# Second feed-forward of a hybrid decoder trunk: one plain f tile ahead of its Strassen units in place of two

## The chip, the cores and the metric

One Trainium2 chip, one of its cores, one launch. The metric is the device time of that core in microseconds (us), the median of several executions. Beside it stands one profiled execution, whose trace the rows below are taken from.

## The reference, cut to what matters

One layer of a decoder trunk on 512 prompt tokens and 64 sample tokens (576 columns in all), in fp32, with D_MODEL = 1024 and D_FF = 2816:

```python
def swiglu(x, w_gu, w_down):
    g, u = jnp.split(x @ w_gu, 2, axis=-1)
    return (jax.nn.silu(g) * u) @ w_down
...
    h = x + 0.5 * swiglu(rms_norm(x, w['g_ffn1']), w['w_ffn1_gu'], w['w_ffn1_down'])
...
    h = h + cross_attend(rms_norm(h, w['g_cross']), mem_k, mem_v, w['w_cq'], w['w_co'])
    h = h + 0.5 * swiglu(rms_norm(h, w['g_ffn2']), w['w_ffn2_gu'], w['w_ffn2_down'])
...
y_prompt = rms_norm(hp, g_final)
```

Only the second feed-forward (`ffn2`) is touched. Its hidden width is 22 tiles of 128, called f tiles here.

## The kernel before, in words

The whole network is one program of five instruction streams (`sync`, `gpsimd`, `tensor`, `scalar`, `vector`) that are written out by hand and meet at semaphores. Activations lie transposed: features on the 128 partitions, 576 tokens along the free axis, 8 chunks (`KD`) of the model width. An fp32 matrix product is made of three fp32r products: every operand is split into a high part (`wh`, `xh`, a copy that rounds to fp32r) and a low part (`wl`, `xl`, the difference), and high x high, high x low and low x high are added up in PSUM.

Weights come in blocks of 1024 x 128, in one order for the whole program (`blocks`); SyncE loads each (`load`) into one of 4 `raw` buffers. For a normal block ScalarE makes `wh` and VectorE makes `wl` (`conv`), and TensorE runs `dense`: 8 chunks x 3 products x 2 halves of 288 columns = 48 matmuls (the line in the profile is that of the helper `mm`, L706). A gate block and an up block belong to each f tile. So a plain f tile is two blocks, 96 matmuls.

In `ffn2` the f tiles behind the first `PLAIN` ones are done as Strassen units. Gate weights, up weights and the two halves of the tokens are combined so that seven products of half the depth take the place of eight: `unit(v)` of TensorE runs A11, S1, A12, S2, S4, A22, S3 with 4 chunks x 3 matmuls each, 84 matmuls of 288 columns. Each unit needs sums of the raw weights. They are made by:

- VectorE, `sum_of`: S1, S2, S4 into PSUM banks 4 to 6 and S3 into SBUF (L2428, L2431, L2438, L2435);
- ScalarE, the high parts: `high_gate` (L1761, A11 and A12 straight from `raw`), `high_sums` (L1769), `high_last` (L1779 and L1781);
- VectorE, the low parts of the sums: `low_sums` (L2444) and `low_last` (L2449);
- GpSimd, the low parts of the straight operands (L694 and L697).

The token side has combinations of its own (`token_sums`, `tokens_high` L1792, `tokens_low` L2458), made once, while the product with `w_co` ahead of `ffn2` runs; the last `tokens_low` is done in the first block of `ffn2`. The scale of the RMS norm, `R`, is also ready only after that block's `rms(3)` (ScalarE L1463 and L1464, VectorE L1946 to L1948).

The 22 f tiles come in three groups of 8, 8 and 6 (`FGROUPS`), each followed by the 8 blocks of its down projection. Before the change the first group is 2 plain tiles and 6 units. In the streams of ScalarE and VectorE the plain blocks are a loop over b: b even multiplies the gate product by `R` (L2494), b odd does the same for the up product (L2500), multiplies by the activation (L2503) and splits the result (L1850, L2509). The preparation of unit 0 hangs on the last plain tile: `high_gate(0)` and the four `sum_of` stand at b = 2 PLAIN - 2, `high_sums(0)` and `low_sums(0)` at b = 2 PLAIN - 1:

```python
                if b % 2 == 0:
                    TTT(two(gs[:]), halves(0), two(R[:]), ALU.mult).then_inc(g_scaled, 1)
                    e.wait_ge(g_scaled, FT + i + 1)
                    e.sem_inc(ps_free, 1)
                    if b:
                        conv(n + 2)
...
                if b == 2 * PLAIN - 2:
                    for j in (S1, S2, S3, S4):
                        sum_of(j, 0)
```

TensorE's unit 0 starts its product A11 when L694 of GpSimd (`lo_a`) is done and the gate product of the last plain tile has been read (`ps_free`), and its product S1 when `low_sums(0)` (`lo_s`) is done. `conv` returns at once for a block that belongs to a unit.

Of the kernel before, what the change touches and what calls it, by code (L numbers as in the profile page):

```python
# [15 lines left out]
KD = D // P  # L16
# [35 lines left out]
def hymba_kernel(nc, A, O, consts):  # L52

    with ExitStack() as ctx:
# [48 lines left out]
        def view(base, at, *dims):  # L103
            n = 1
            for d in dims:
                n *= d
            v = base[:, at:at + n]
            if len(dims) == 1:
                return v
            names = "abcd"[:len(dims)]  # L110
            return v.rearrange(f"p ({' '.join(names)}) -> p {' '.join(names)}",
                               **{k: d for k, d in zip(names[1:], dims[1:])})
# [106 lines left out]
        ROWS = dict(prompt=(1, 2, 4, 5), decode=(3, 6))  # L219
        EXPS = dict(prompt=(4, 8, 13, 17), decode=(9, 18))  # L220
        TURNS = dict(prompt=(1, 2, 3, 5), decode=(4, 6))
        HK, PLAIN = KD // 2, 2
        xg = view(MM, 7168, HK, T)
        tok_h, tok_l = view(ARr, 0, HK, 4, TH), view(ARr, 8 * T, HK, 4, TH)
        tok_hf, tok_f = tok_h.bitcast(F32), view(AR, 8 * T, HK, 4, TH)
# [2402 lines left out]
```

## Time and profile before

| | |
|---|---|
| median of 3 runs | 1312.79 us (1312.44 to 1313.26) |
| the profiled execution | 1314.22 us |
| its span in the trace | 1312.4 us |
| mean granted TensorE clock | 0.998 of full speed |
| TensorE busy | 1290.7 us, 98% of the span |
| TensorE weight loads | 1251.4 us, beside the matmuls |
| VectorE busy | 763.1 us, 58% |
| ScalarE busy | 480.0 us, 37% |
| GpSimd busy | 359.4 us, 27% |
| the chain that ended last | TensorE 93%, VectorE 3%, ScalarE 2% |

The span leaves out about 1.8 us of the execution's own time. Rows name an instruction by line, engine, operation and "out<-in". In this stretch of the program `ARr` and `AR` are one buffer that holds the combined operands and tokens, `gua` holds gate, up and activation, `PS` is PSUM, and `raw` the loaded weights. A wait is shown in brackets in front of the instruction that waited, with the instruction that released it.

### The profile page before, as it was taken

Reading aid. Unit: us, or ns where it says so; the run is one execution under the profiler, and the core shown is the slowest. Engines: PE = TensorE matmul, PEld = TensorE weight load, DVE = VectorE, ACT = ScalarE, POOL = GpSimd, SP = SyncE. Lnnn points to the kernel's source line nnn. Section 1 sums busy time; section 2 is a strip of 40 time slices with the busy share of each in tenths; the row PEclk is TensorE's granted clock in tenths of the full one; section 3 lists DMA queues with packets and bytes.
Section 4 is the critical chain, followed back from the end, with each engine's and each line's share of the span. In section 5 each row is a group of like instructions: output and inputs, shape, how many; then the busy total and the mean of one; then the engine's idle time right before and its main releaser. Section 6 shows DMA issues by size and latency. Waiting matters only on the chain.

```text
span 1312.4 us, 24249 instructions
## 1 busy us (share of the span) xinstructions
PE 1290.7 (98%) x10419; PEld 1251.4 (95%) x10419; DVE 763.1 (58%) x934; ACT 480.0 (37%) x709; POOL 359.4 (27%) x428
## 2 busy tenths in 40 slices
PE   7999999999999999999999999999999999999998
PEld 6999999999999999999999997599999999999997
DVE  3535345653644645648665536568795389737953
ACT  6322122221223423455343313245453245413543
POOL 0000789988901302000002100021330033103321
PEclk9999999999999999999999999999999999999999
DMA  6543222222222352124433546422233233323221
GB/s 174 112 101 98 81 79 83 81 81 82 80 85 70 89 101 64 51 73 131 130 89 106 177 163 255 161 65 81 82 95 96 80 97 91 89 81 97 85 61 72
DMA packets 227147, 130.24 MB, mean 99 GB/s; under 512 B 22241, under 2 KB 221393, under 8 KB 227025
## 3 DMA queue, kind: packets, MB, share of 16 engines
q1 hardware_dynamic: 223168, 123.66, 32.8%
q10 hardware_dynamic: 3872, 5.04, 1.1%
q8 instruction: 82, 1.34, 0.4%
q14 instruction: 25, 0.20, 0.0%
HBM read 121.72 MB, written 5.78 MB: 97 GB/s over the span
## 4 chain that ended last, share of the span: by engine, by line
PE 93%; DVE 3%; ACT 2%; issue 1%; DMA 1%; SPq 0%; DVEq 0%; ACTq 0%
PE PS L706 89%; PE PS L1245 1%; DMA AR<-in_x_prompt 1%; PE PS L781 0%; PE PS L1331 0%; ACT wh L1430 0%; ACT gua L1488 0%; DVE Hs L2123 0%; DVE ARr L2444 0%; PE PS L1223 0%; PE PS L863 0%; PE PS L1196 0%; DVE xl L2449 0%; DVE wl L1904 0%; DVE PS L2428 0%
## 5 line engine op out<-in xcount | busy, mean ns | idle before, releaser
L1430 ACT ACTIVATE wh<-raw 128x1024 fp32r<-128x1024 f32 (+1 forms) x152 | 157.7, 1037 | 522.1 <-PE PS L706 521.9
L706 PE MATMUL PS<-xh,wh 128*128 128x288 f32 x1152 | 254.1, 302 | 0.3 <-DVEq L2496 0.2
L706 PE MATMUL PS<-xh,wl 128*128 128x288 f32 x1152 | 247.1, 296 | 0.0
L706 PE MATMUL PS<-xl,wh 128*128 128x288 f32 x1152 | 246.8, 296 | 0.0
L1904 DVE TENSOR_TENSOR wl<-raw,wh 128x1024 fp32r<-128x1024 f32 (+1 forms) x152 | 197.1, 1297 | 67.1 <-ACT wh L1430 66.3
L706 PE MATMUL PS<-yh,wh 128*128 128x288 f32 x960 | 206.5, 297 | 0.0
L706 PE MATMUL PS<-yh,wl 128*128 128x288 f32 x960 | 205.5, 296 | 0.0
L706 PE MATMUL PS<-yl,wh 128*128 128x288 f32 x960 | 205.5, 296 | 0.0
L706 PEld LDWEIGHTS PS<-xh,wh 128*128 128x128 f32 x1152 | 185.3, 190 | 3.1 <-issue 1.5
L706 PEld LDWEIGHTS PS<-xl,wh 128*128 128x128 f32 x1152 | 185.9, 189 | 0.0
L706 PEld LDWEIGHTS PS<-xh,wl 128*128 128x128 f32 x1152 | 185.9, 189 | 0.0
L706 PEld LDWEIGHTS PS<-yh,wh 128*128 128x128 f32 x960 | 154.4, 189 | 1.3 <-DVE yl L2376 0.8
L706 PEld LDWEIGHTS PS<-yh,wl 128*128 128x128 f32 x960 | 154.7, 189 | 0.0
L706 PEld LDWEIGHTS PS<-yl,wh 128*128 128x128 f32 x960 | 154.7, 189 | 0.0
L497 POOL TENSOR_TENSOR acc<-acc,sq 128x576 f32<-128x576 f32 x31 | 52.4, 1692 | 322.8 <-issue 163.4
L510 POOL TENSOR_TENSOR AR<-AR 128x32 f32<-128x32 f32 (+6 forms) x184 | 116.3, 632 | 14.8 <-POOL AR L623 0.4
L706 PE MATMUL PS<-xh,ARr 128*128 128x288 f32 x480 | 105.9, 296 | 0.1
L694 POOL TENSOR_TENSOR ARr<-raw,ARr 128x1024 fp32r<-128x1024 f32 x20 | 55.1, 2756 | 113.4 <-ACT ARr L1761 113.4
L706 PEld LDWEIGHTS PS<-xh,ARr 128*128 128x128 f32 x480 | 80.3, 188 | 0.4 <-ACT sq L1808 0.4
L706 PE MATMUL PS<-ARr 128*128 128x288 f32 x480 | 70.0, 295 | 3.6 <-DVE ARr L2444 3.6
L706 PE MATMUL PS<-xl,ARr 128*128 128x288 f32 x240 | 70.9, 295 | 0.0
L706 PEld LDWEIGHTS PS<-ARr 128*128 128x128 f32 x480 | 65.5, 188 | 4.3 <-DVE ARr L2444 4.3
(364 smaller groups left out, 1804.1 us busy)
## 6 DMA issues: line engine op xcount, KB each, us to landing
raw<-in_w_ffn_gu SPq DMA_DIRECT2D x88, 512.0 KB, 3.9
raw<-in_w_ffn_down SPq DMA_DIRECT2D x32, 512.0 KB, 3.9
raw<-in_w_in SPq DMA_DIRECT2D x16, 512.0 KB, 4.1
raw<-in_w_ckv SPq DMA_DIRECT2D x16, 512.0 KB, 3.9
raw<-in_w_ffn_down SPq DMA_DIRECT2D x16, 384.0 KB, 3.4
Hs<-in_cache_mem_k SPq DMA_DIRECT2D x6, 1024.0 KB, 6.3
raw<-in_w_out SPq DMA_DIRECT2D x8, 512.0 KB, 3.9
raw<-in_w_cq SPq DMA_DIRECT2D x8, 512.0 KB, 4.3
```

Of the source, the lines that this page charges most:

```text
L497: e.tensor_tensor(acc[:, 0:T], acc[:, 0:T], sq[:, k % 2, :], ALU.add).then_inc(acc_ready, 1)
L510: own(TTT(o, a, b, ALU.mult))
L694: TTT(operands(v, A11, 2, 1), raw[:, n % 4, :].rearrange("p (s x) -> p s x", s=2), operands(v, A11, 2, 0).bitcast(F32), ALU.subtract).then ...
L706: return e.matmul(out, lhsT, rhs, start=start, stop=stop, **kw)
L1245: last = e.transpose(bank(4 + q % 3, P, at=f * M + j * P), KB[b][:, j, at:at + P], ident)
L1430: e.activation(wh[:, n % 2, 0:K * P], raw[:, n % 4, 0:K * P], ACT.Copy).then_inc(w_hi, 1)
L1904: TTT(wl[:, n % 2, 0:K * P], raw[:, n % 4, 0:K * P], wh[:, n % 2, 0:K * P].bitcast(F32), ALU.subtract).then_inc(w_lo, 1)
```

## The change

One number: how many f tiles of the first group are plain.

```diff
@@ -219,7 +219,7 @@
         ROWS = dict(prompt=(1, 2, 4, 5), decode=(3, 6))
         EXPS = dict(prompt=(4, 8, 13, 17), decode=(9, 18))
         TURNS = dict(prompt=(1, 2, 3, 5), decode=(4, 6))
-        HK, PLAIN = KD // 2, 2
+        HK, PLAIN = KD // 2, 1
         xg = view(MM, 7168, HK, T)
         tok_h, tok_l = view(ARr, 0, HK, 4, TH), view(ARr, 8 * T, HK, 4, TH)
         tok_hf, tok_f = tok_h.bitcast(F32), view(AR, 8 * T, HK, 4, TH)
```

The second f tile becomes a unit: the first group is 1 plain tile and 7 units, `FIRST_UNIT` goes from 0, 6, 14, 20 to 0, 7, 15, 21, the two blocks of that tile are no longer split by `conv`, and the preparation of unit 0 moves from b = 2 and 3 to b = 0 and 1.

VectorE, from the last step of `rms(3)` to the third of the four sums, before the change:

```order
L1948 SCALAR_TENSOR_TENSOR R<-gua,R 128x576
L1904 TENSOR_TENSOR wl<-raw,wh 128x1024
L2458 TENSOR_TENSOR ARr<-AR,ARr 128x864
L2494 TENSOR_TENSOR gua<-PS,R 128x576
L2500 TENSOR_TENSOR gua<-PS,R 128x576
L2503 TENSOR_TENSOR gua<-gua 128x576
L1904 TENSOR_TENSOR wl<-raw,wh 128x1024
L2509 TENSOR_TENSOR yl<-gua,yh 128x576
L2494 TENSOR_TENSOR gua<-PS,R 128x576
L2428 TENSOR_TENSOR PS<-raw 128x512
L2431 TENSOR_TENSOR PS<-PS,raw 128x512
L2435 TENSOR_TENSOR AR<-raw 128x512
```

and with the change, from the same step to `low_sums(0)` (L2444) and one row on:

```order
L1948 SCALAR_TENSOR_TENSOR R<-gua,R 128x576
L2458 TENSOR_TENSOR ARr<-AR,ARr 128x864
L2494 TENSOR_TENSOR gua<-PS,R 128x576
L2428 TENSOR_TENSOR PS<-raw 128x512
L2431 TENSOR_TENSOR PS<-PS,raw 128x512
L2435 TENSOR_TENSOR AR<-raw 128x512
L2438 TENSOR_TENSOR PS<-PS,raw 128x512
L2500 TENSOR_TENSOR gua<-PS,R 128x576
L2503 TENSOR_TENSOR gua<-gua 128x576
L2444 TENSOR_TENSOR ARr<-PS,ARr 128x3x512
L2509 TENSOR_TENSOR yl<-gua,yh 128x576
```

Both `wl` splits and one round of L2494, L2500, L2503 and L2509 are gone from here, and the four sums stand right behind the first gate product.

ScalarE, from the last step of its `rms(3)` on, as a difference:

```order
 L1464 ACTIVATE R<-R 128x576
 L1792 ACTIVATE ARr<-AR 128x864
-L1430 ACTIVATE wh<-raw 128x1024
+L1761 ACTIVATE ARr<-raw 128x2x512
 L1845 ACT_TABLE_LOAD
 L1845 ACTIVATE gua<-gua 128x576
-L1430 ACTIVATE wh<-raw 128x1024
+L1769 ACTIVATE ARr<-PS 128x3x512
 L1850 ACTIVATE yh<-gua 128x576
-L1761 ACTIVATE ARr<-raw 128x2x512
-L1845 ACTIVATE gua<-gua 128x576
-L1769 ACTIVATE ARr<-PS 128x3x512
```

`high_gate(0)` (L1761), which GpSimd's L694 waits for, stands where the `wh` of the third block stood, in front of the table load.

## Rows read from the trace of the kernel before

**Rows 1.** Waits of TensorE from 895 to 1265 us (us in total, times, longest).

```profile
PE PS L706 <- DVE ARr L2444: 3.6, 3, 1.7
```

**Rows 2.** Timeline of TensorE (start, length, matmuls, in brackets idle time and releaser).

```profile
916.11 0.51 PE L706 MATMUL PS<-xh,wh 128*128 128x288 f32 x2 [0.22 <-DVEq L2496]
...
928.67 0.30 PE L706 MATMUL PS<-xh,ARr 128*128 128x288 f32 x1
...
932.14 1.85 PE L706 MATMUL PS<-ARr 128*128 128x288 f32 x12 [1.71 <-DVE ARr L2444]
...
940.91 0.53 PE L706 MATMUL PS<-ARr,xh 128*128 128x288 f32 x2 [0.57 <-ACT sq L1808]
```

**Rows 3.** Stretches: length, then busy time of each engine, clock, DMA share, GB/s.

```profile
916.11:928.67 12.56, 12.56 (x96) 12.56 (x97) 6.71 (x9) 5.24 (x6) 2.40 (x1) 1.00 0.36 101
950.00:961.15 11.15, 11.15 (x86) 11.15 (x85) 10.38 (x13) 6.13 (x11) 4.11 (x2) 1.00 0.33 95
```

**Rows 4.** Timeline of VectorE from the scale R to the first low sums.

```profile
912.25 0.76 DVE L1948 SCALAR_TENSOR_TENSOR R<-gua,R 128x576 f32<-128x576 f32 x1
913.04 1.23 DVE L1904 TENSOR_TENSOR wl<-raw,wh 128x1024 fp32r<-128x1024 f32 x1
914.18 1.05 DVE L2458 TENSOR_TENSOR ARr<-AR,ARr 128x864 fp32r<-128x864 f32 x1
915.15 0.75 DVE L2494 TENSOR_TENSOR gua<-PS,R 128x576 f32<-128x576 f32 x1
...
922.63 0.76 DVE L2494 TENSOR_TENSOR gua<-PS,R 128x576 f32<-128x576 f32 x1 [3.13 <-PE PS L706]
...
928.87 0.76 DVE L2500 TENSOR_TENSOR gua<-PS,R 128x576 f32<-128x576 f32 x1 [2.64 <-PE PS L706]
...
930.34 1.75 DVE L2444 TENSOR_TENSOR ARr<-PS,ARr 128x1536 fp32r<-128x1536 f32 x1
```

**Rows 5.** Timeline of ScalarE in the same stretch.

```profile
911.35 1.04 ACT L1430 ACTIVATE wh<-raw 128x1024 fp32r<-128x1024 f32 x1
...
918.23 1.04 ACT L1761 ACTIVATE ARr<-raw 128x1024 fp32r<-128x1024 f32 x1
...
926.27 1.46 ACT L1769 ACTIVATE ARr<-PS 128x1536 fp32r<-128x1536 f32 x1 [2.16 <-DVE PS L2438]
```

**Rows 6.** The page's DMA issues: count, KB each, us to landing.

```profile
raw<-in_w_ffn_gu SPq DMA_DIRECT2D x88, 512.0 KB, 3.9
```

**Rows 7.** Timeline of GpSimd.

```profile
885.40 1.99 POOL L497 TENSOR_TENSOR acc<-acc,sq 128x576 f32<-128x576 f32 x1 [4.41 <-ACT sq L1456]
...
919.35 2.40 POOL L694 TENSOR_TENSOR ARr<-raw,ARr 128x1024 fp32r<-128x1024 f32 x1 [12.84 <-ACT ARr L1761]
```

**Rows 8.** Timeline of VectorE beside the first of them, and 8 us later.

```profile
885.29 0.81 DVE L1937 SCALAR_TENSOR_TENSOR xl<-h,gains,xh 128x576 fp32r<-128x576 f32 x1
886.02 1.69 DVE L2467 SCALAR_TENSOR_TENSOR AR<-h,gains,AR 128x288 f32<-128x288 f32 x1
...
894.25 0.50 DVE L2467 SCALAR_TENSOR_TENSOR AR<-h,gains,AR 128x288 f32<-128x288 f32 x1
```

**Rows 9.** Stretches as in rows 3; the clock stands behind POOL's busy time.

```profile
928.00:932.00 4.00, 2.43 (x19) 2.19 (x17) 3.10 (x3) 1.55 (x3) 0.00 (x0) 1.00 0.35 104
1302.00:1303.00 1.00, 1.00 (x10) 0.97 (x10) 0.34 (x2) 0.27 (x1) 0.00 (x0) 1.00 0.00 0
1304.00:1305.00 1.00, 0.80 (x4) 0.37 (x3) 0.96 (x2) 1.00 (x2) 0.00 (x0) 0.50 0.00 0
```

**Rows 10.** Timeline of TensorE at the start of the program.

```profile
14.01 0.68 PE L706 MATMUL PS<-xl,wh 128*128 128x288 f32 x2
14.49 0.68 PE L706 MATMUL PS<-xh,wl 128*128 128x288 f32 x2
...
20.10 0.43 PE L706 MATMUL PS<-xh,wl 128*128 128x288 f32 x2
```

## Prediction

> **What bounds the kernel now.** I read the engines' shares first: TensorE is busy 98% of the span and has 93% of the chain that ended last, so only two things can move the time here, how many matmuls there are and how long TensorE stands still between them. Then its waits in the second feed-forward. The reader is to see how few they are: three waits for the low sums, L2444, 3.6 us together [rows 1], of which 1.71 us belong to unit 0; then 0.22 us in front of the second plain tile and 0.57 us inside unit 0 for an eviction by ScalarE [rows 2]. Last, the timelines of VectorE, ScalarE and GpSimd from 911 to 932 us, because the change moves the preparation of unit 0 there. What matters is which engine reaches `low_sums(0)` last, since TensorE's product S1 hangs on it.
>
> **The matmuls.** The second plain tile is 96 matmuls in 12.56 us; a unit in the middle of the group takes 11.15 us from one to the next, TensorE busy all of that time [rows 3]. The change swaps one for the other: 12.56 - 11.15 = 1.41 us less. The unit that comes in stands among steady ones; VectorE is busy 10.38 us of its 11.15 us, so it doesn't bound it, and the first and the last unit keep their waits. The Trainium skill ("TensorE: Matmul & The Clock Gate", Back-to-back issue gap) gives an isolated matmul of N columns N / 2.4 + 2.5 ns at full clock, 122.5 ns for 288, from which 12 fewer would be an estimated 1.47 us less. The trace has 131 and 133 ns for one [rows 3], and the sum goes by the trace.
>
> **When unit 0 can start.** Before, unit 0 was prepared beside the second plain tile. Now only what TensorE does up to 915.89 us (916.11 less 0.22, the end of the first tile) covers it. Nothing of it could start much sooner, since the first gate product waits for the scale R, and R comes off VectorE at 913.0 us [rows 4]. I follow the new order from there, in times of the old trace.
>
> 1. ScalarE. L1761 takes the place of the `wh` copy at 911.35 us, same size, 1.04 us [rows 5]. Its input is loaded: a load lands 3.9 us after issue [rows 6], and its buffer was free from the split of the block four places earlier, with three blocks of 48 x 0.133 = 6.4 us between.
> 2. GpSimd. Before, it took up L694 1.12 us after L1761 began (918.23 to 919.35) and needed 2.40 us [rows 5, 7]. Now it asks at 911.35 + 1.12 = 912.47 us, while VectorE is in L1948, which reads two inputs from SBUF [rows 4].
> 3. Who waits for whom there is the term that decides. The trace has the pattern once already: GpSimd's L497 was issued at 885.40 us inside VectorE's L1937 and took 1.99 us, and VectorE's next instruction with two SBUF inputs, L2467, took 1.69 us where it takes 0.50 us 8 us later; it ended at 887.71, 0.32 us after GpSimd [rows 7, 8]. So the instruction under way ends, GpSimd goes first, and VectorE stands still until it is done. By that row GpSimd starts in earnest at 913.0 and ends at 913.0 + 2.40 = 915.4 us.
> 4. VectorE. The split `wl` at 913.04 us is gone, which by itself brings the rest forward by 914.18 - 913.04 = 1.14 us. But L2458, now issued at 913.04, also has two SBUF inputs. It is held until 915.4 and needs 0.8 us more (0.97 us alone, less the 0.18 us that L2467 had behind it). The gate product L2494 so starts at 916.15 us, 1.0 us later than before (915.15) and not 1.1 us sooner. Price of the hold: 2.1 us. Its other end is 0, if VectorE gets in first or the two don't meet. I take 2.1, by the row that has the same two engines in the same order.
> 5. TensorE. Before, L2494 at 915.15 released it at 916.11, 0.96 us later [rows 2, 4]. Now A11 of unit 0 starts at 916.15 + 0.96 = 917.1 us: a wait of 1.2 us in place of 0.22.
> 6. The sums. From the start of L2494 to that of L1769 on ScalarE it was 926.27 - 922.63 = 3.64 us, with the same four sums between [rows 4, 5]. Now L1769 starts at 919.8 and ends at 921.25. VectorE does L2500 and L2503 meanwhile (1.5 us, 919.65 to 921.2), whose inputs are ready, so `low_sums(0)` begins at 921.3. From there to TensorE's S1 it was 932.14 - 930.34 = 1.80 us [rows 2, 4]. S1 starts at 923.1 us.
> 7. A11 itself runs 1.76 us (928.67 to 932.14 less 1.71), to 918.9 us. The wait in front of S1 is then 4.2 us in place of 1.71.
>
> **The sum.** From 915.89 us to S1 it was 16.25 us and becomes 7.2, 9.05 us less; the unit that comes in adds 11.15. Net +2.1 us. The same by terms: -1.41 for the matmuls, +1.0 for the first wait, +2.5 for the second. Behind S1 I cost nothing: VectorE, ScalarE and GpSimd go through the same instructions at the same distances from `low_sums(0)`, the 0.57 us wait in unit 0 stays, weights of unit 1 are loaded earlier than before, and the down blocks and the later groups are unchanged but for which of two operand buffers a unit uses.
>
> The profiled execution took 1314.22 us, 1.8 us more than its span and 1.4 more than the median of 1312.79. On its own time the sum gives 1316.3; against the median 1312.8 + 2.1 = **1314.9 us**, 0.16% more. A measurement of this kernel can tell about 0.2%, 2.6 us, from no change.
>
> **Rivals.**
>
> *TensorE's clock falls in the new wait (slower).* The granted clock is 1.00 through the 1.71 us wait [rows 9]. At the end of the program it goes from 1.00 at 1302 us to 0.50 at 1304, that is from 2.4 to 1.2 GHz, after the dense blocks had given way to short transposes and waits [rows 9]. The new stretch from 915.9 to 923.1 has 1.76 us of matmuls and waits of 1.2 and 4.2 us, longer than any other in this trace behind the start. If the clock falls there, S1 and what follows run at half rate for a while. At the start of the program two matmuls took 0.48 us (14.01 to 14.49) where two take 0.26 in the plain tile [rows 3], and the slow pace was over by 20.10 [rows 10]. 6.1 us at that pace cost 6.1 x (1 - 0.133 / 0.24) = 2.7 us, of which the 0.57 us wait in unit 0 can swallow a part: 2.1 us, between ends of 0 and 2.7. Time: 1312.8 + 2.1 + 2.1 = 1317.0, with the upper end at 1317.6. It decides from the point where the sum plus the loss passes 2.6 us, so from a loss of 0.5 us. Against it: I can't tell from the trace how long a wait must be.
> The Trainium skill ("TensorE: Matmul & The Clock Gate", HAM oscillation) says that gaps between bursts of matmuls put the clock back to half, to be earned again, every time. By it this rival would be the rule rather than the exception for 4.2 us. The end of the trace agrees that light work lets the clock fall; no row shows it for a wait of this length between dense matmuls.
>
> *GpSimd and VectorE don't meet (no change).* If L694 is taken up a little later, or VectorE's L2458 gets in first, L2494 starts at 914.0 us, `low_sums(0)` at 919.15, S1 at 920.95, and A11 right at 915.9. Then 16.25 - 5.06 = 11.19 us less against 11.15 more: 1312.8 us. For it speaks that the margin is 0.6 us (912.47 against 913.04); against it the pattern of rows 7 and 8.
>
> *The waits don't grow at all (faster).* Then only the 1.41 us of matmuls show, 1311.4 us. It would need unit 0 to be prepared before R is there, and in the new order the sums stand behind the gate product; I see nothing for it. That the number doesn't do what it says is excluded by the new order, which has seven units in the first group.
>
> **How the numbers follow.** The forecast 0.50, the clock 0.32, no meeting 0.13, other causes 0.05 (mostly further waits in the first two units). The predicted time is that of the forecast, 1314.9. The range takes in the case without the hold at its low end, 1312.5, and the clock at its high end, most of the way to 1317.6: 1317.4. Slower by over 0.2%, above 1315.4: nearly all of the clock's share, and a little of the forecast's and of the rest, 0.37. Within 0.2%: 0.60. Faster by over 0.2% would need 2.6 us where the change removes 1.4 us of matmuls: 0.03.
>
> **What would show it.** Right: GpSimd's L694 for unit 0 at about 912.5 us with about 2.9 us on the record, L2458 beside it with 2.9 to 3.2 us in place of 1.05, L2494 at 916.1, then TensorE waiting about 1.2 us for L2494 and 4.2 us for L2444; seven units with 11.15 us between the middle ones. Wrong: L2458 of about 1.05 us (the hold is no cost), matmuls 0.24 us apart behind S1 with a granted clock under 1.00 (the clock), new waits in units 1 to 6, or a steady unit over 11.15 us.

## The result and the profile after

The changed kernel takes 1315.33 us (median of 11 runs, 1314.46 to 1315.91), the kernel before 1312.55 us in the runs beside it (11 runs, 1310.55 to 1314.99). The ratio is 1.0020, with a 95% interval of 1.0010 to 1.0029: 2.8 us slower, between 1.3 and 3.8. The prediction was 1314.9, 2.1 us slower.

The profiled execution took 1315.53 us, with a span of 1313.7 us. The page's first part, its busy times:

```profile
PE 1288.3 (98%) x10407; PEld 1250.2 (95%) x10407; DVE 770.7 (59%) x940; ACT 484.3 (37%) x715; POOL 362.3 (28%) x430
```

TensorE has 12 matmuls fewer (10407 for 10419) and 2.4 us less busy time (1290.7 before), and the kernel is slower all the same. Its waits from 895 to 1265 us, which answer to [rows 1]:

```profile
PE PS L706 <- DVE ARr L2444: 6.0, 3, 4.1
PE PS L706 <- DVEq L2496: 1.1, 1, 1.1
```

The waits for low sums grew from 3.6 to 6.0 us, all of it in the longest one. The timeline of TensorE at the places of [rows 2]:

```profile
914.94 0.37 PE L706 MATMUL PS<-xh,ARr 128*128 128x288 f32 x1 [1.14 <-DVEq L2496]
...
920.92 3.25 PE L706 MATMUL PS<-ARr 128*128 128x288 f32 x12 [4.15 <-DVE ARr L2444]
```

The two waits are there, 1.14 and 4.15 us. But the twelve matmuls behind the second (product S1) take 3.25 us where they took 1.85: the clock. And the third wait of the rows before, 0.57 us for ScalarE in unit 0, is gone. The stretches around it, read as [rows 9]:

```profile
915.00:918.00 3.00, 1.77 (x12) 1.54 (x12) 2.97 (x5) 0.83 (x2) 0.00 (x0) 1.00 0.00 0
918.00:921.00 3.00, 0.08 (x1) 0.08 (x1) 2.90 (x4) 3.00 (x6) 0.12 (x1) 0.84 0.61 175
921.00:924.00 3.00, 3.00 (x13) 3.00 (x14) 3.00 (x3) 1.04 (x2) 3.00 (x2) 0.50 0.05 13
924.00:927.00 3.00, 3.00 (x14) 3.00 (x14) 3.00 (x3) 0.41 (x1) 1.45 (x1) 0.52 0.58 167
927.00:930.00 3.00, 3.00 (x25) 3.00 (x24) 1.48 (x3) 1.75 (x2) 0.00 (x0) 1.00 0.29 83
```

The columns are as in [rows 3]. TensorE stood still from 916.8 us. In that stillness the granted clock fell to 0.50 (1.2 GHz), was there while 27 matmuls ran in 6 us, and was at 1.00 from 927 us on, where 25 go into 3 us. The mean granted clock was 0.996 or 0.997 in the 11 runs of the changed kernel. In the 66 runs of the kernel before that stood beside the experiments it was 0.997 in 20, 0.998 in 38, 0.999 in 8 and never 0.996, with the change 0.996 in 6 of 11: lower on the whole, but a mean of 0.997 doesn't tell for a single run whether the clock fell here.

What made the wait so long stands on VectorE (first block, as [rows 4]), ScalarE and GpSimd (as [rows 5, 7]):

```profile
910.15 0.76 DVE L1948 SCALAR_TENSOR_TENSOR R<-gua,R 128x576 f32<-128x576 f32 x1
910.95 3.13 DVE L2458 TENSOR_TENSOR ARr<-AR,ARr 128x864 fp32r<-128x864 f32 x1
914.00 0.74 DVE L2494 TENSOR_TENSOR gua<-PS,R 128x576 f32<-128x576 f32 x1
...
919.11 1.76 DVE L2444 TENSOR_TENSOR ARr<-PS,ARr 128x1536 fp32r<-128x1536 f32 x1
```

```profile
909.26 1.05 ACT L1761 ACTIVATE ARr<-raw 128x1024 fp32r<-128x1024 f32 x1
```

```profile
910.38 2.78 POOL L694 TENSOR_TENSOR ARr<-raw,ARr 128x1024 fp32r<-128x1024 f32 x1 [5.97 <-ACT ARr L1761]
```

GpSimd's L694 was issued 0.23 us after VectorE's L1948 had begun, and was done at 913.16, which is 2.25 us after that ended. VectorE's next instruction, L2458, took 3.13 us for 1.05 and ended 0.92 us after GpSimd. What marks the instructions that are held can be read from the same trace: L2431, with one input in PSUM and one in SBUF, took 0.69 to 0.70 us in all 21 units, also beside GpSimd; L2435, of the same size with both inputs in SBUF, took 0.68 us in the fastest and 1.20 in the median.

**A zero point.** In this trace everything up to here happens 2.1 us earlier than in the one of before. The difference is there in full 30 us into the program and stays the same from then on; against the second trace of before (below) the first is off by 1.75 us in the same way, so it belongs to the execution and not to the kernel. What exactly differs in that start was not taken apart. Spans therefore can't be compared to better than some 2 us. From here on times are counted from the mean-square product of `rms(3)`, the last thing both kernels do alike, to the last residual update (L2563). These four rows are its ends, of the kernel before and then of the changed one, from the timelines of TensorE and VectorE:

```profile
906.56 1.29 PE L706 MATMUL PS<-acc,mean_d 128*128 128x512 f32 x4
...
1299.45 0.76 DVE L2563 SCALAR_TENSOR_TENSOR h<-PS,h 128x576 f32<-128x576 f32 x1 [5.44 <-PE PS L706]
```

```profile
904.47 1.29 PE L706 MATMUL PS<-acc,mean_d 128*128 128x512 f32 x4
...
1300.74 0.76 DVE L2563 SCALAR_TENSOR_TENSOR h<-PS,h 128x576 f32<-128x576 f32 x1 [5.44 <-PE PS L706]
```

That is 392.89 us before and 396.27 after, 3.4 us more. The end of the program behind it took between 12.9 and 14.0 us in the traces, whatever the kernel. All traces on this scale, with the ratio of the timed runs to the kernel before:

```
kernel                               to S1   S1 to S2   to last residual   ratio, 95% interval
before                               25.58   3.28       392.89
before, second trace                 25.87   3.29       393.19
changed                              16.45   5.93       396.27             1.0020 (1.0010 to 1.0029)
changed, second trace                16.47   4.83       395.15
e1 gate first                        14.39   4.81       393.08             1.0002 (0.9993 to 1.0011)
e2 28 matmuls in the wait            16.46   3.29       394.99             1.0013 (1.0004 to 1.0022)
e3 both                              14.39   3.29       392.93             0.9997 (0.9988 to 1.0005)
e4 three plain tiles                 38.68   3.28       393.65 (*)         1.0004 (0.9995 to 1.0012)
e5 low sums first (two plain)        24.00   3.18       391.05 (*)         0.9990 (0.9981 to 0.9998)
e5, second trace                     23.98   3.18       392.22
e6 and the eviction first            24.01   3.18       392.22             0.9989 (0.9980 to 0.9998)
e7 sums first (one plain)            12.45   3.27       391.96             0.9994 (0.9985 to 1.0003)
e8 14 matmuls in the wait            16.46   3.27       394.96             1.0015 (1.0006 to 1.0024)
(*) 8 down blocks at 6.24 us each where all others have 6.40: 1.3 us, see the end
```

### The profile page after: what moved, and what is told of

The parts are those of the page before. It is cut to its first block, busy times and chain, and to the rows that moved or that the text cites. A ratio compares the mean times of both kernels' runs of the same rounds, so it can differ in the third digit from the quotient of the medians.

```text
span 1313.7 us, 24248 instructions
## 1 busy us (share of the span) xinstructions
PE 1288.3 (98%) x10407; PEld 1250.2 (95%) x10407; DVE 770.7 (59%) x940; ACT 484.3 (37%) x715; POOL 362.3 (28%) x430
## 4 chain that ended last, share of the span: by engine, by line
PE 94%; DVE 3%; ACT 2%; issue 1%; DMA 1%; SPq 0%; DVEq 0%; ACTq 0%
PE PS L706 90%; PE PS L1245 1%; DMA AR<-in_x_prompt 1%; DVE ARr L2444 0%; PE PS L781 0%; ACT wh L1430 0%; ACT gua L1488 0%; DVE Hs L2123 0%; PE PS L1223 0%; PE PS L863 0%; PE PS L1196 0%; PE PS L1331 0%; DVE ARr L2458 0%; DVE AR L2578 0%; PE PS L874 0%
## 5 line engine op out<-in xcount | busy, mean ns | idle before, releaser
L706 PE MATMUL PS<-xh,wh 128*128 128x288 f32 x1120 | 246.6, 302 | 0.1
L706 PE MATMUL PS<-xh,wl 128*128 128x288 f32 x1120 | 240.2, 296 | 0.0
L706 PE MATMUL PS<-xl,wh 128*128 128x288 f32 x1120 | 239.6, 296 | 0.0
L706 PEld LDWEIGHTS PS<-xh,wh 128*128 128x128 f32 x1120 | 179.8, 189 | 2.5 <-issue 1.1
L706 PEld LDWEIGHTS PS<-xh,wl 128*128 128x128 f32 x1120 | 180.6, 189 | 0.0
L706 PEld LDWEIGHTS PS<-xl,wh 128*128 128x128 f32 x1120 | 180.4, 189 | 0.0
L706 PE MATMUL PS<-xh,ARr 128*128 128x288 f32 x504 | 112.3, 299 | 1.1 <-DVEq L2496 1.1
L706 PEld LDWEIGHTS PS<-xh,ARr 128*128 128x128 f32 x504 | 85.3, 190 | 1.3 <-issue 1.3
L694 POOL TENSOR_TENSOR ARr<-raw,ARr 128x1024 fp32r<-128x1024 f32 x21 | 56.3, 2680 | 109.3 <-ACT ARr L1761 109.3
L706 PE MATMUL PS<-ARr 128*128 128x288 f32 x504 | 74.9, 298 | 6.0 <-DVE ARr L2444 6.0
L706 PEld LDWEIGHTS PS<-ARr 128*128 128x128 f32 x504 | 70.2, 191 | 6.7 <-DVE ARr L2444 6.7
```

The source lines that it names most:

```text
L694: TTT(operands(v, A11, 2, 1), raw[:, n % 4, :].rearrange("p (s x) -> p s x", s=2), operands(v, A11, 2, 0).bitcast(F32), ALU.subtract).then ...
L706: return e.matmul(out, lhsT, rhs, start=start, stop=stop, **kw)
```

## The experiments

The theory after the result: the hold of VectorE by GpSimd costs 2.1 us, which is the whole forecast, since without it the longer wait would cost just what the 12 matmuls give; on top of it comes the fallen clock. The rivals: the hold is harmless, since something else sets S1; and the clock's loss is swallowed by slack.

**e1, gate first.** On ScalarE, `high_gate(0)` of the changed kernel goes in front of `rms(3)`:

```diff
                 if b == 0:
+                    high_gate(0)
                     rms(3)
                     tokens_high(KD - 1)
                 conv(n0 + b + 2)
-                if b == 2 * PLAIN - 2:
-                    high_gate(0)
```

> The changed kernel with one instruction of ScalarE moved: high_gate(0) (L1761) in front of rms(3) and no longer behind tokens_high, so that GpSimd does its L694 before VectorE gets to the scale R. Theory A (the hold costs 2.1 us): L2458 behind R falls from 3.13 to about 1.05 us, the gate product L2494 starts 1.8 us behind R's L1948 where it was 3.85, S1 on TensorE 8.7 us behind L1948 where it was 10.8. The wait in front of S1 becomes about 3.4 us. Against the changed kernel 2.1 us less, 1313.2, if the clock still falls; 3.4 us less, 1311.9 (the time before is 1312.6), if it doesn't. Rival B (the hold was harmless, something else sets S1): L2458 shorter but S1 still near 10.8 us behind L1948, time 1315.3. The hold may turn up in L2467 to L2469, where VectorE has about 2 us to spare.

S1 came 2.06 us sooner, and the last residual 3.2 us sooner than in the first trace of the changed kernel. Against its second trace, in which S1 to S2 takes 4.83 us as it does here (4.81), it is 2.07 us. VectorE's timeline (the experiment's line numbers are 1 less):

```profile
904.29 2.64 DVE L2466 SCALAR_TENSOR_TENSOR AR<-h,gains,AR 128x288 f32<-128x288 f32 x1
...
910.29 1.06 DVE L2457 TENSOR_TENSOR ARr<-AR,ARr 128x864 fp32r<-128x864 f32 x1
911.26 0.75 DVE L2493 TENSOR_TENSOR gua<-PS,R 128x576 f32<-128x576 f32 x1
```

L2458 is back at 1.06 us. The hold didn't vanish, it moved: the token sum now in its way takes 2.64 us for 0.50, in a stretch where VectorE afterwards waits for R anyway. So the hold costs what lies on the path at that moment, and theory A stands. The clock still fell, behind a wait of 3.44 us, but for a shorter time (S1 to S2 4.81 us).

**e2, 28 matmuls in the wait.** On TensorE, between A11 and the wait for S1 of unit 0. They write a bank that nobody reads, so nothing of the computation changes:

```diff
+                if v == 0:
+                    for i in range(28):
+                        mm(bank(0, TH), operand(0, A11, 0)[:, i % HK, :], xh[:, i % HK, lo_t])
                 e.wait_ge(S("lo_s"), 2 * v + 1)
```

> The changed kernel with 28 extra matmuls of 288 columns on TensorE between A11 and the wait for S1 of unit 0, into a bank that nobody reads; they fit in the wait (28 x 0.133 = 3.7 of 4.15 us). Theory A (the fall of the clock costs 1.3 us net): granted clock stays at 1.00 from 915 to 935 us, S1 still 10.8 us behind L1948, S1 to S2 takes 3.3 us where it took 5.9, the 0.57 us wait for ScalarE in unit 0 comes back, and the time is 1.3 us below the changed kernel, about 1314.0. Rival B (the clock's loss is all slack of unit 0): same time as the changed kernel, 1315.3.

The waits of TensorE in its timeline:

```profile
915.85 0.37 PE L706 MATMUL PS<-xh,ARr 128*128 128x288 f32 x1 [1.16 <-DVEq L2499]
...
921.82 1.85 PE L706 MATMUL PS<-ARr 128*128 128x288 f32 x12 [0.41 <-DVE ARr L2447]
...
930.60 0.53 PE L706 MATMUL PS<-ARr,xh 128*128 128x288 f32 x2 [0.56 <-ACT sq L1811]
```

S1 is where it was, and runs in 1.85 us again; the clock is 1.00 in all stretches from 915 to 930 us, and the 0.56 us wait for ScalarE is back. To the last residual it is 1.28 us less than in the first trace of the changed kernel. The timed runs can't tell that from nothing: 1.0013 against 1.0020, with intervals that overlap. What they do say is that the kernel with its clock at full speed is still slower than before: what is left is 2.1 us in the trace, 1.7 (0.5 to 2.9) in the runs.

**e3, both**, with 24 extra matmuls:

> Both edits together, with 24 extra matmuls. Theory A (hold 2.1 us and clock 1.3 us are separate and are all that was lost beyond the swap of 96 matmuls for 84): 3.4 us below the changed kernel, 1311.9, so level with the kernel before at 1312.6 or 0.1 us under it. Rival B (they overlap, or a third wait takes over): more than 1 us above the kernel before.

392.93 us to the last residual, 3.3 below the first trace of the changed kernel and level with the kernel before at 392.89. The two losses add up, 2.06 (e2 to e3) and 1.28 (changed to e2). That it is level, and not below, is the cover that went with the tile: without the hold TensorE stands still for 3.44 us in front of S1 (e1) where it was 0.22 + 1.71, 1.5 us more, as much as the swapped matmuls give.

**e4, three plain tiles**, the opposite step from the kernel before (`PLAIN = 3`):

> The opposite step from the kernel before: three plain tiles ahead of five units. With the preparation of unit 0 covered as before, the waits stay at 0.22, 1.71 and 0.57 us, the clock stays at 1.00 and only the matmuls count: 12.56 - 11.15 = 1.4 us more than before, 1314.0. Rival (the 1.71 us wait of unit 0 is not the same when another tile covers it): not between +0.9 and +1.9 us.

The waits were the same, 0.22, 1.73 and 0.56 us, and the clock stayed up. The runs give +0.5 us (-0.7 to +1.6), in line with 1.4. The trace gives S1 13.10 us later for one unit of 11.15 us less: 1.95 us, more than the forecast, because the two plain tiles between the first and unit 0 took 25.65 us here, 133 ns a matmul, and the one of rows 3 took 12.56, 131 ns. That trace is the only one to have it so: in the other four with two plain tiles the second took as long as here. The total of +0.76 us is about that less 1.3 us for the faster down blocks.

**e8, 14 matmuls in the wait**, e2 with `range(14)`:

> The changed kernel with 14 extra matmuls, 1.9 us of the 4.15 us wait, right behind A11, so that a wait of about 2.3 us is left in front of S1. Theory A (a wait of this length doesn't let the clock fall, as the 1.71 us one did not): clock 1.00 throughout, S1 to S2 3.3 us, and 408.0 us from the mean-square product to the end. Rival B (the two waits together bring it down, whatever stands between): S1 to S2 4.5 us or more.

```profile
920.77 1.85 PE L706 MATMUL PS<-ARr 128*128 128x288 f32 x12 [2.28 <-DVE ARr L2447]
```

With a wait of 2.28 us left, S1 runs in 1.85 us and the clock is 1.00: theory A. In the trace half of the filler does all that the full one does. It is one trace; the mean clock of the 10 timed runs is 0.996 in two of them, 0.997 in seven and 0.999 in one, so it isn't shown that the clock stayed up in each. And the filler did two things, it shortened the wait and gave TensorE more work in front of it; which of them counts was not separated.

**Second traces**, of the kernel before, the changed one and (below) e5:

> The kernel before once more, for a second trace. In the first one the 8 down blocks behind the first group of units took 6.40 us each, in the trace with low_sums(0) moved 6.24 us, although the matmuls are the same. Theory A (each execution falls into one pace or the other by chance): a different pace may show here. Rival B (the pace belongs to the program): 6.40 us again, and 12.56 us for the second plain tile.

> The changed kernel once more. The hold (L2458 at 3.1 us), the wait of 4.15 us in front of S1 and the granted clock of 0.50 behind it come back if they belong to the change and not to one execution: 16.45 us from the mean-square product to S1, 5.9 us from S1 to S2 within 1 us. Theory A on the pace: 6.24 or 6.40 us a down block; rival B: 6.40 again.

The hold (L2458 at 3.14 us), the two waits (1.16 and 4.14 us) and the fall came back. But the clock was low for less long, and it fell only when S1 had begun, at 921.14 us; the stretches as above:

```profile
918.00:921.00 3.00, 0.00 (x0) 0.00 (x0) 2.89 (x3) 3.00 (x5) 0.00 (x0) 1.00 0.62 173
921.00:924.00 3.00, 2.86 (x12) 2.86 (x13) 3.00 (x4) 1.26 (x3) 2.91 (x2) 0.54 0.04 8
924.00:927.00 3.00, 3.00 (x22) 3.00 (x21) 3.00 (x3) 0.41 (x1) 1.67 (x1) 0.89 0.65 174
```

S1 to S2 took 4.83 us for 3.29, a loss of 1.5 us instead of 2.65, and to the last residual it is only 0.16 us more than in e2. So about 1.4 us of the loss are free. Where they go can be read from the starts of S1 of units 0, 1 and 2, at 921.82, 933.88 and 945.43 us in e2 and at 921.14, 933.91 and 945.04 us here. With the clock up the units take 12.06 and 11.55 us and the later ones 11.17, so the first two have 0.9 and 0.4 us more than TensorE needs; here they take 12.77 and 11.13, and 1.25 us of the loss are made up when unit 2 gets to S1. The same shows between e1 and e3, 1.5 us of loss and 0.15 us of price. The second trace of before had the second plain tile at the slower pace (S1 0.29 us later) and down blocks at 6.40 us.

**Can unit 0 be prepared better?** e5 takes the kernel before (two plain tiles) and does `low_sums(0)` right behind the four sums, in front of the last up product:

```diff
-                    if b == 2 * PLAIN - 1:
-                        low_sums(0)
...
                 if b == 2 * PLAIN - 2:
                     for j in (S1, S2, S3, S4):
                         sum_of(j, 0)
+                    low_sums(0)
```

> The kernel before (two plain tiles) with one step of VectorE moved: low_sums(0) (L2444) in front of the last up product L2500, right behind the four sums. Its 1.71 us wait on TensorE should nearly vanish, because L2500 there waits 2.64 us for TensorE with low_sums(0) queued behind it. Theory A (VectorE's queue behind it sets unit 0): S1 starts about 1.6 us sooner, but VectorE gets to the sums of unit 1 only 0.2 us sooner, since it waits for ScalarE's yh; TensorE's wait for ScalarE's eviction L1808 in unit 0 grows from 0.57 to about 2.0 us, and from the mean-square product of rms(3) to the end it is 405.6 us, against 405.8 before. Rival B (the wait in front of S1 is paid in full): 404.2 us and 1.6 us less time.

> The kernel before with low_sums(0) moved, once more. Theory A: the down blocks behind the first group may be at 6.40 us now, and then it is 405.3 us from the mean-square product to the end, 0.5 less than the kernel before. Rival B: 6.24 us again and 404.1 us.

The timeline of TensorE, first trace:

```profile
939.73 0.53 PE L706 MATMUL PS<-ARr,xh 128*128 128x288 f32 x2 [1.61 <-ACT sq L1808]
```

The 1.71 us wait in front of S1 is gone and 1.0 us of it turned up again in front of ScalarE's eviction, which stands in ScalarE's queue behind sums that VectorE makes late: 1.6 us for 0.57. At equal pace (second traces) 0.97 us are left of the gain, and the timed runs confirm a gain: 0.9990 (0.9981 to 0.9998). My 0.2 us was too low, since `low_sums(1)` came 1.0 us sooner (33.35 us behind the mean-square product for 34.33, second traces).

e6 adds, on ScalarE in unit 0, the eviction in front of `high_sums(1)`:

```diff
+                if v == 0:
+                    keep(v, 4, e2, u_bank(v))
                 high_sums(after(v)) if after(v) else conv(units[v] + 3)
-                keep(v, 4, e2, u_bank(v))
+                if v:
+                    keep(v, 4, e2, u_bank(v))
```

> As the one with low_sums(0) moved, and on ScalarE the eviction keep(0, 4) (L1808) of unit 0 in front of high_sums(1) (L1769), so that S3 of unit 0 no longer waits for VectorE's sums of unit 1. Theory A: neither wait is left, S1 of unit 1 waits about 0.5 us for its own low sums, and from the mean-square product to the end it is 403.7 us, 2.1 us less than the kernel before. Rival B (only the eviction's order counted): 0.6 us less, 405.2.

```profile
941.17 1.81 PE L706 MATMUL PS<-ARr 128*128 128x288 f32 x12 [0.67 <-DVE gua L2552]
...
947.27 0.40 PE L706 MATMUL PS<-xh,ARr 128*128 128x288 f32 x1 [1.10 <-ACT sq L1808]
```

Theory A fell. Rival B's number came true against the first trace of before (0.67 us less, 0.6 expected), but not its reason: against e5 the eviction's new place gives nothing. The wait in unit 0 is gone, and two new ones in unit 1, 0.67 and 1.10 us, bring the last residual back to 392.22, to the hundredth where e5's second trace has it. The preparation of unit 1 is what sets it: from `low_sums(0)` to `low_sums(1)` it is 12.05 us here and the same in e5. That is not VectorE alone; 2.3 us of it VectorE waits for ScalarE (0.82 for the high part of the hidden tile, 1.52 for `high_sums(1)`), and S3's sum, beside GpSimd, takes 2.29 us for 0.68. The hold is on this path too.

e7 takes the changed kernel (one plain tile) and reorders all of it; the core of it on VectorE and TensorE:

```diff
+            rms(3)
+            for j in (S1, S2, S3, S4):
+                sum_of(j, 0)
...
             TTT(two(gs[:]), halves(0), two(R[:]), ALU.mult).then_inc(g_scaled, 1)
...
             TTT(two(us[:]), halves(2), two(R[:]), ALU.mult).then_inc(ps_free, 1)
+            low_sums(0)
+            tokens_low(KD - 1)
...
             TTT(us[:], us[:], act[:], ALU.mult).then_inc(hid, 1)
...
-                if first:
+                if first and v:
                     e.wait_ge(ps_free, seq(n) + 1)
```

> The changed kernel (one plain tile, seven units) with unit 0 prepared in another order. VectorE behind R: the four sums, gate product, up product, low_sums(0), and only then tokens_low, the product with the activation and the low part yl. ScalarE: high_gate(0) in front of rms(3), high_sums(0) in front of the activation, high_last(0) and the first eviction in front of yh, keep(0, 4) in front of high_sums(1). TensorE starts A11 of unit 0 without waiting for the gate product, whose banks it doesn't use. Expected, by durations of the trace: S1 12.4 us behind the mean-square product (changed kernel 16.45), a wait of about 1.5 us in front of it, clock at 1.00, no wait inside unit 0, and 402.9 us from the mean-square product to the end, 2.9 less than the kernel before and 6.3 less than the changed one. Rival: VectorE's work behind R is the bound whatever its order; then a wait of more than 1 us turns up in unit 0 or 1 and it is above 404.

```profile
916.46 1.85 PE L706 MATMUL PS<-ARr 128*128 128x288 f32 x12 [1.54 <-DVE ARr L2440]
...
928.52 1.81 PE L706 MATMUL PS<-ARr 128*128 128x288 f32 x12 [0.69 <-DVE gua L2537]
...
934.62 0.40 PE L706 MATMUL PS<-xh,ARr 128*128 128x288 f32 x1 [1.10 <-ACT sq L1808]
```

Everything up to the end of unit 0 went as worked out (S1 at 12.45 us, expected 12.4), and then the rival came true: the same two waits in unit 1. 391.96 us, 1.2 below the second trace of before instead of the 2.9 expected. Preparing unit 0 earlier brought TensorE up to the pace at which VectorE and ScalarE prepare unit 1 (11.32 us from `low_sums(0)` to `low_sums(1)`) and no further. In the timed runs it can't be told from the kernel before, 0.9994 (0.9985 to 1.0003). e5 and e6, with two plain tiles, are the versions that beat the kernel before, by 0.1%; the changed kernel is a further 0.2% behind.

## Why the prediction was right, and where it was not

- **The matmuls, -1.41 us.** The right term with a row that flattered the plain tile. It ran at 131 ns a matmul; the second trace of before has 12.86 us from tile start to A11 for 12.56. The swap is worth 1.4 to 1.7 us, as the pace falls out, and 1.7 is the more usual.
- **GpSimd asks inside L1948 and goes first (steps 2 and 3).** Right: L694 was issued 1.12 us behind the start of L1761, inside L1948, and had 2.78 us on the record, 2.9 forecast.
- **The hold, 2.1 us (step 4).** Right: L2458 3.13 us; e1 and e3 give 2.06 us back.
- **The waits, 1.2 and 4.2 us (steps 5 to 7).** Right: 1.14 and 4.15. S1 came 16.45 us behind the mean-square product; the forecast of 923.1 us in the times of the old trace is 16.5.
- **Nothing behind S1.** Right with the clock at full speed: e2, whose clock stays up, is 2.10 us above the kernel before (1.8 above its second trace), where the sum says 2.1.
- **The clock.** This is the step that failed. The forecast with half of the chance had the clock stay at 1.00; it fell in both traces of the changed kernel, and the mean clock of the 11 runs is lower than before on the whole. I gave that rival 0.32, because the trace of before had no wait of this length between dense matmuls, and bounded it well: 0 to 2.7 us, taken as 2.1. It measured 2.65 us and 1.5 us of loss, of which 1.28 and 0.16 us reached the end. The Trainium skill ("TensorE: Matmul & The Clock Gate", HAM oscillation), by which such gaps between bursts put the clock back to half, was the better guide here: the traces agree with it for the waits of 4.15, 4.14 and 3.44 us. What I didn't have is the slack behind: I let only the 0.57 us wait swallow a part, and it was about 1.4 us.
- **The total.** 2.1 + 0.2 to 1.3 gives 2.3 to 3.4 us by the traces (0.3 less against the second trace of before), 2.8 in the runs. The time lay inside the range, near the forecast, though by a sum with one term more. That it lay so near is in part luck: without the slack, which I hadn't seen, the clock's 1.5 to 2.65 us would have come on top in full. The direction, slower or level and not faster, was right for its reason: the two waits eat more than the matmuls give, and as e3 shows it is the hold that makes it more and not just as much.

## What to carry to other kernels

Fewer instructions on the busiest engine can be worth nothing where the work taken out was the cover under which the next stage was prepared: cost the swap as a timeline of every queue from the last fixed event (here the scale R) to the first instruction that waits, not as a difference of counts. On the path, look for instructions of VectorE with two SBUF inputs beside one of GpSimd (here 3.13 us for 1.05); the start times told here who gets in first, and moving the one that isn't urgent cost one line. And when a wait grows past those in the trace, allow for TensorE's clock, then ask how much slack lies behind before charging it in full.

## What the runs showed that I had not expected

**The clock.** It fell in or just behind waits of 4.15, 4.14 and 3.44 us, and stayed at 1.00 with waits of 1.5 (e7), 1.7 and 2.28 us at the same place. In front of each TensorE had run product A11, 12 matmuls, behind the dense block; in front of the 2.28 us it had run 14 more. How long it stayed low differed in two traces of the same kernel: 5.93 and 4.83 us from S1 to S2.

**Two paces of the same matmuls at full clock.** The down blocks behind the first group of units, 48 matmuls each, take 6.40 us apiece in 11 of the 13 traces, and 6.24 in e4 and in the first trace of e5, with the granted clock at 1.00 in both. The same stretch in the two traces of e5, first and second:

```profile
1015.00:1045.00 30.00, 30.00 (x233) 30.00 (x232) 11.20 (x13) 5.40 (x6) 2.48 (x1) 1.00 0.27 79
```

```profile
1015.00:1045.00 30.00, 30.00 (x227) 30.00 (x227) 10.94 (x13) 6.33 (x6) 2.48 (x1) 1.00 0.25 72
```

233 matmuls against 227 in 30 us, one program, two executions. So the pace doesn't belong to the program. What sets it was not found. Over eight blocks it is worth 1.3 us, as much as the 12 matmuls that the change removes, and it may be one reason why runs of one kernel spread over 1.5 to 4.4 us (not shown; only single executions were traced). A single trace can't price a change of this size by its span.
